# Attentions and mlps by 256 tokens, the first half beside the expert rows of the second

## What is computed

```python
def peer_ffn(u, w_q, sub_keys, expert_u, expert_v):
...
        ue = jnp.take(expert_u, expert, axis=0)
        ve = jnp.take(expert_v, expert, axis=0)
        h = jax.nn.gelu(jnp.einsum('thkd,td->thk', ue, xc).astype(F32), approximate=False)
        return jnp.einsum('thk,thkd->td', (gate * h).astype(xc.dtype), ve)
...
    for l in range(DEPTH_2):
...
            h = h + diff_attention(hn, w_qkv_a[l], w_o_a[l], lambda_q1[l], lambda_k1[l],
                                   lambda_q2[l], lambda_k2[l], subln_g[l], lambda_init,
                                   cos_a, sin_a)
...
            h = h + mla_attention(hn, w_dq[j], q_norm_g[j], w_uq[j], w_o_b[j],
                                  k_nope, k_rope, v, cos_b, sin_b)
        h = h + sq_relu_mlp(rms_norm(h, mlp_norm_g[l]), w_up[l], w_down[l])
    return rms_norm(h, final_norm_g)
```

## Time and profile before

| | us |
|---|---|
| median of 3 runs | 3588.33 |
| lowest, highest | 3582.31, 3590.96 |
| the profiled execution | 3589.93 |
| its span, first to last instruction | 3588.1 |
| TensorE busy | 2908.2 |
| DVE busy | 2067.9 |
| POOL busy | 1356.3 |
| ACT busy | 691.9 |
| mean granted TensorE clock | 0.921 |

### The profile page before, as it was taken

One profiled execution on the slowest core, in us unless ns is written; L12 is line 12 of the kernel. 1 busy time (PEld: TensorE's weight loads), 2 busy tenths in 40 slices (PEclk: granted clock), 3 DMA queues, 4 the chain that ended last, 5 costly groups with the idle time before them and its releaser, 6 DMA issues.

```text
span 3588.1 us, 31787 instructions
## 1 busy us (share of the span) xinstructions
PE 2908.2 (81%) x11588; PEld 1975.4 (55%) x11588; DVE 2067.9 (58%) x4063; ACT 691.9 (19%) x1259; POOL 1356.3 (38%) x764
## 2 busy tenths in 40 slices
PE   4954798695777777787777765999799997899998
PEld 3743788573332332333222222786688886677887
DVE  6798543446785777678665544336453444455334
ACT  2101222121000000000000002234232233343221
POOL 3833222245454444444444423320144442123442
PEclk9966999797999999999999987987799998899999
DMA  6210001125999999999999973210022213112221
GB/s 256 94 47 12 1 1 41 54 106 220 421 419 421 401 421 409 403 422 408 420 421 421 419 309 132 71 71 1 28 94 102 94 48 115 36 50 92 94 98 43
DMA packets 97691, 692.13 MB, mean 193 GB/s; under 512 B 10752, under 2 KB 10880, under 8 KB 14848
## 3 DMA queue, kind: packets, MB, share of 16 engines
q0 software_dynamic: 73728, 536.90, 36.3%
q1 hardware_dynamic: 23808, 153.20, 11.8%
HBM read 687.96 MB, written 2.10 MB: 192 GB/s over the span
## 4 chain that ended last, share of the span: by engine, by line
PE 53%; DMA 22%; DVE 16%; issue 5%; POOL 2%; ACT 2%; DVEq 0%; SPq 0%; ACTq 0%; POOLq 0%
PE ps L1775 10%; DMA w<-in_peer_uv,un 9%; PE ps L306 8%; PE ps L1623 8%; PE ps L1754 8%; DMA raw<-in_peer_uv,un 7%; PE ps L781 5%; DMA un<-in_peer_uv,un 5%; DVE scratch L559 4%; PE ps L2037 3%; PE ps L1967 2%; PE ps L2059 1%; DVE scratch L1678 1%; PE ps L1945 1%; PE ps L335 1%
## 5 line engine op out<-in xcount | busy, mean ns | idle before, releaser
L276 POOL TENSOR_TENSOR wl<-raw,wh 128x2048 fp32r<-128x2048 f32 (+2 forms) x118 | 530.9, 4507 | 1122.1 <-ACT wh L270 1121.9
L1623 PE MATMUL ps<-w,un 128*128 128x512 f32 x856 | 415.4, 632 | 159.3 <-DVE un L1686 159.3
L1623 PE MATMUL ps<-raw,un 128*128 128x512 f32 x768 | 376.6, 638 | 121.6 <-DVE un L1686 121.6
L1623 PEld LDWEIGHTS ps<-w,un 128*128 128x128 f32 x856 | 164.2, 200 | 405.3 <-DVE un L1686 228.9
L1678 DVE SCALAR_TENSOR_TENSOR scratch<-w,scratch 128x1024 f32<-128x1024 f32 x214 | 265.8, 1253 | 184.1 <-DMA w<-in_peer_uv,un 184.1
L1611 POOL DMA_INDIRECT w<-in_peer_uv,un x214 | 248.5, 1161 | 320.7 <-PE ps L1623 294.5
L1623 PEld LDWEIGHTS ps<-raw,un 128*128 128x128 f32 x768 | 147.9, 202 | 347.1 <-DVE un L1686 189.7
L1611 POOL DMA_INDIRECT raw<-in_peer_uv,un x192 | 235.8, 1228 | 263.9 <-PE ps L1623 251.3
L1678 DVE SCALAR_TENSOR_TENSOR scratch<-raw,scratch 128x1024 f32<-128x1024 f32 x192 | 232.8, 1223 | 137.8 <-DMA raw<-in_peer_uv,un 137.5
L1651 ACT ACTIVATE un<-un 128x2 f32<-128x2 f32 x256 | 52.1, 203 | 1224.5 <-DVE scratch L1678 1224.4
L270 ACT CAST wh<-raw 128x2048 fp32r<-128x2048 f32 (+2 forms) x118 | 216.9, 1851 | 317.4 <-PE ps L1775 194.7
(11 more groups left out here) (385 smaller groups left out, 5256.6 us busy)
## 6 DMA issues: line engine op xcount, KB each, us to landing
raw<-in_w_up SPq DMA_DIRECT2D x32, 1024.0 KB, 4.8
raw<-in_w_down SPq DMA_DIRECT2D x32, 1024.0 KB, 4.8
scratch<-in_ada_w SPq DMA_DIRECT2D x13, 1024.0 KB, 14.6
raw<-in_w_qkv_a SPq DMA_DIRECT2D x12, 1024.0 KB, 5.3
raw<-in_w_in SPq DMA_DIRECT2D x11, 1024.0 KB, 5.6
raw<-in_ada_w SPq DMA_DIRECT2D x11, 1024.0 KB, 4.8
raw<-in_peer_w_q SPq DMA_DIRECT2D x8, 1024.0 KB, 7.0
raw<-in_w_out SPq DMA_DIRECT2D x4, 1024.0 KB, 6.0
```

Of the source, the lines that this page charges most:

```text
L276: e.tensor_tensor(self.wl[h][:, 0:width], self.raw[slot][:, 0:width], self.wh[h][:, 0:width].bitcast(F32), ALU.subtract).then_inc(*self.ti ...
L1623: ins = e.matmul(self.ps[:, b + half, :], self.diag[n % 8], self.rows[self.row_of(n)][:, 1024 + 512 * half:1536 + 512 * half], start=k == ...
```

## The change

**Two halves.** The tail is written anew for 256 tokens (`Half`, `h` = 0 or 1) and runs twice, one half after the other (`pe_tail` and its siblings). Matmuls, activations and DVE instructions are 256 columns wide. The weight tiles are 128 x 1024 (in part 768), 184 per half, and every half loads, casts and splits all of them, through four `raw` buffers and four slots, in the mlps seven. The keys and values of half 0 go to HBM and come back for half 1. POOL's part in the double norm goes to DVE.

**Rows.** The first 256 rows run beside the three choices, 2.6 rows per step (`with_rows`, `beside`). The last 256 run beside the tail of half 0, 1.1 rows per unit of its weight (a unit is 24 matmuls of 256 columns; a step of attention counts 1.2; the whole is 242 units). From row 236 on there are six buffers. The rows' products change engine: the diagonal is made on ACT; of the last 256 rows three in four are multiplied and summed on DVE into SBUF (`acc`) and one in four on TensorE (`on_pe`), and DVE adds the two sums up (`dve_sums`). ACT makes Gelu and gate for one row at a time, in two instructions. POOL's splits stand between its row transfers, as soon as the slot is free by the order of turns (`spot`).

```diff
-LAST_RAW = 480
+FEW_ROWS = 236
+RATE = 1.1
...
+         "w_qk": (1024, 16, 8), "w_v": (1024, 8, 4), "w_o_a": (1024, 8, 8), "w_dkv": (1024, 3, 8), "ukv_k": (1024, 2, 2),
+         "ukv_v": (1024, 2, 2), "w_dq": (1024, 3, 8), "uq_n": (768, 4, 3), "uq_r": (768, 2, 3), "w_o_b": (1024, 8, 8),
+         "w_up_0": (1024, 32, 8), "w_up_1": (1024, 32, 8), "w_down_0": (1024, 32, 1), "w_down_1": (1024, 32, 1)}
...
+    for h in range(2):
+        for key in tail_keys(h):
+            plan[key] = (len(plan), 4 + len(plan) % 4, None)
...
+        slots = (4, 5, 6, 7, 8, 9, 10) if name[0:4] in ("w_up", "w_do") else (4, 5, 6, 7)
+        slot = min(slots, key=lambda s: -1 if last[s] is None else plan[last[s]][0])
+        before[key], last[slot] = last[slot], key
+        plan[key] = plan[key][0:2] + (slot,)
...
-        return n % 10 if n < LAST_RAW else (n - LAST_RAW) % 6
+        return n % 10 if n < FEW_ROWS else 4 + (n - FEW_ROWS) % 6
...
+    def on_pe(n):
+
+        return n < 256 or n % 4 == 3
...
-    def with_gather(self, choose, gather):
-
-        for tt in range(1, 4):
-            for n, _ in enumerate(choose(tt)):
-                for _ in range(2 if n % 2 else 1):
-                    next(gather)
-            for _ in range(64 - 46):
-                next(gather)
-        for _ in gather:
...
+    def beside(self, stage, rows, rate):
+
+        due = 0.0
+        for weight in stage:
+            self.turn += 1
+            due += rate * (weight or 1)
+            while due >= 1:
+                next(rows, None)
+                due -= 1
...
+    def with_rows(self, choose, rows, tail):
+
+
+        early = itertools.islice(rows, 257)
+        self.beside(itertools.chain(choose(1), choose(2), choose(3)), early, 2.6)
+        for _ in early:
             pass
+        self.banks, self.nbank = 6, 0
+        self.beside(tail(self.halves[0]), rows, RATE)
+        for _ in rows:
+            pass
+        self.banks, self.nbank = NBANK, 0
+        for _ in tail(self.halves[1]):
+            self.turn += 1
...
+            while n >= FEW_ROWS + 12 and at < len(lows) and self.spot_before(lows[at]) <= self.spot.get(("row", before), 0):
+                self.pool_lo(e, lows[at])
+                at += 1
...
+        e.activation(self.gelus[:, c], self.dots[:, c], ACT.Gelu, bias=0.0, scale=1.0).then_inc(*self.tick(S))
+        e.wait_ge(*self.last(S))
+        e.activation(self.weight[:, c], self.gelus[:, c], ACT.Identity, bias=0.0,
+                     scale=self.gate[n // 128][:, k:k + 1]).then_inc(*self.tick(S, ("weight", n)))
...
+            e.activation(self.diag[self.diag_of(n)], self.C("ident"), ACT.Identity, bias=0.0,
+                         scale=self.weight[:, c]).then_inc(*self.tick(S, ("diag", n)))
...
-                e.tensor_scalar(self.diag[n % 8], self.C("ident"), self.gelus[:, n % 256:n % 256 + 1],
-                                self.gate[tt][:, k:k + 1], ALU.mult, ALU.mult).then_inc(*self.tick(S, ("diag", n)))
...
+                    e.wait_ge(*self.at(S, ("acc", n - 1 if not self.on_pe(n - 1) else n - 2)))
+                    e.scalar_tensor_tensor(out=acc, in0=v, scalar=w, in1=acc, op0=ALU.mult,
+                                           op1=ALU.add).then_inc(*self.tick(S, ("acc", n)))
...
+            if n == 384:
+                self.dve_sums(e, 2)
...
+        blocks = [(hh, qb) for hh in range(8) for qb in (2 * H.h, 2 * H.h + 1)]
...
+                        for n, (l, r) in enumerate(self.terms(wh[:, k, :], wl[:, k, :], *H.B[k])):
+                            ins = e.matmul(self.ps[:, b, 0:256], l, r, start=k == 0 and n == 0, stop=k == 7 and n == 2)
...
+        yield from self.pe_joined(e, H)
+        yield from self.pe_diff(e, H)
+        yield from self.pe_mlp(e, H, 0)
+        yield from self.pe_mla(e, H)
+        yield from self.pe_mlp(e, H, 1)
+        yield from self.pe_final(e, H)
```

1591 lines of the change are left out of this document (865 added, 726 removed).

## The result

The changed kernel takes 3847.9 us (median; 3843.0 to 3850.4) against 3585.3 for the kernel before: 1.074 times as long, 95% interval 1.070 to 1.079. 3690 had been forecast, slower by 2.8%. The sign was right and the time lies in the range, but the loss was given as 105 us and is 263. The profiled execution took 3849.6 us, its span 3847.8.

The account below looks back on a forecast made before the run. DMA bound the rows and TensorE the tail, in series; side by side, the DVE/POOL port would bind. 1515 us to the 256th row + 1336 stage + 835 tail 1 = 3686, rounded 3690 with surroundings; range 3450 to 3870.

Parts of the forecast that it names:

- The bound before, and what both halves share: Rows bound by DMA, tail by TensorE, in series; side by side, DVE's two-SBUF-tensor instructions and POOL's splits exclude each other.
- The sum of 1135 us: Second rows beside tail 0: 542 us of dots and sums, 433 of splits, 160 of the half tail's DVE instructions, added.
- 256th row at 1515: First 256 rows run as before to 1510 us, plus 5 us for six buffers from row 236.
- Resources: Second rows beside tail 0, each resource's sum: DMA 871 us, TensorE 700, POOL 740, DVE 850.
- what doesn't pack: Second rows beside tail 0, added to the port's sum: attention 81 us, latencies 40, order 80.
- Order: POOL, ACT and TensorE wait for one another: 46 us per mlp group, 8% above the sum, 80 us in all.
- Tail 1 835: Last 256 tokens alone: 526 us matmuls, 154 attentions, 123 latencies, 32 splits; 835 us, between 800 and 880.
- split bursts: Tail 1's mlps: splits arrive in bursts of five, 13 us within 11.5, costing 2 us a group, 32 in all.
- the port doesn't add up: Rival: splits slip between dots or DVE's sums are free; stage some 1070 us, end 3425; chance 0.17.
- it packs well: Rival: port times add but order costs nothing; stage 1220 us, whole 3547, deciding at 1238 for the stage; chance 0.15.
- The third: Rival: TensorE's lower clock makes groups 56 us, whole 3850; or dots wait for POOL's row issues, 3930; chance 0.16.

Follow-up runs that it names:

- e1: Changed kernel with POOL splitting only 64 of 1024 columns for nearly every tail weight tile; 3512.1 us, 0.981 of the kernel before.
- e4: Changed kernel with all 368 splits of the tails' weights on DVE in place of POOL; 3813.0 us, 1.065 of the kernel before.
- e2: Changed kernel with RATE 0: the last 256 rows run behind the first half tail, not beside it; 3836.2 us, 1.072 of the kernel before.
- e12: Changed kernel with splits of 64 columns and dots and weights of rows 256 to 511 one row further ahead; 3413.5 us, 0.954 of the kernel before.
- e15: Changed kernel: first tail's and three of eight later splits on DVE, every second late row on TensorE, dots one row ahead, Gelu per two rows; 3567.3 us, 0.996.
- e5: Changed kernel with dots and weights of rows 256 to 511 two rows further ahead; 3837.8 us, 1.071 of the kernel before.
- e3: Changed kernel with all of rows 256 to 511 summed on TensorE, not one in four; 3825.0 us, 1.070 of the kernel before.

## Why the prediction was right or wrong

- **The bound before, and what both halves share.** Right. The step "DVE and POOL exclude each other, so their times add" is what e1 shows, 294 us of holding on DVE in the stage. The sum of 1135 us was 1082, so 5% too high. Of the signs named, mlp groups at 50.5 us for 46, DMA at 69% for 65 and 84 table loads for some 80 came near; dots and sums had means of 1.48 and 1.90 us and a longest of 4.1, for 2 and over 5.
- **256th row at 1515.** 1520. The splits of the tail's first four tiles were not in the step. POOL ran them in one go ahead of a row's issue, and a dot was held until they were over (in e4, where DVE splits them later, the dot of row 256 starts at 1512.5 us, here at 1520.3). DVE's work up to there was 474 us for 480, though no row shows the 110 us in its working, where its own subtraction gives 73:

```profile
1479.47 10.91 DVE L1748 SCALAR_TENSOR_TENSOR scratch<-un,scratch 128x1024 f32<-128x1024 f32 x1 [1.25 <-DMA un<-in_peer_uv,un]
...
1480.07 9.23 POOL L297 TENSOR_TENSOR wls<-raws,whs 128x1024 fp32r<-128x1024 f32 x4
```

- **Resources.** DVE 850: 827 in e1. POOL 740: 786 as it ran, its own waiting included. TensorE 700: 891; e2 has 670 of it for the tail alone and 240 for the 64 rows, which is 3.75 us a row at a granted clock of 0.59, in place of the 2.0 of before. DMA: 369 MB for 362. None of these sums is as long as the stage.
- **The step that failed: what doesn't pack.** The terms of 81 + 40 + 80 = 201 us measured 401. "Order", 8% on the bound resource, was the worst. The 16 groups of the mlps were to take 736 us, 678 of port and 58 beside it (46 a group, 3.6 of it beside the port); they took 809, 630 of port and 179 beside it (11.2 a group). The attentions, 213 us with 81 beside the port, took 242 with 125 beside it. The rest, with 62 beside the port, had 97. The port's term was 53 us too high and hid part of this; 200 less 53 is the 147 us by which the stage was missed. What stands in place of a percentage is a ring of waits of its own: TensorE waits for a row's diagonal, ACT for its dot, DVE behind a split or an activation. TensorE stands in it for 20 us of each group. e12 measures a part of it with the port nearly out of the way: one row of lead, 99 us.
- **Tail 1 835.** 845. Its groups took 27.2 us for 25; 97 us of it hang on the splits (e1), not 32 as "split bursts" had it. Other terms were too high by some 55 us, the attentions among them (135 for 154). So 835 was near by two errors that offset each other.
- **What should have been asked, and wasn't.** The forecast set the stage against its resources, and never against its two parts run one behind the other. By its own terms these are 645 us for the transfers and 526 + 71 + 123 + 32 = 752 for the half tail (71 being 225 less 154 of attention), 1397 together. So even the forecast's 1336 left an overlap of only 61 us, against the 190 that halving costs by the same terms (752 + 835 less 1397.5). Measured, the parts are 652 + 815 = 1467 and halving costs 263.
- **The rivals.** The first (the port doesn't add up, 3425) falls by e1. The second (it packs well, 3547) did not come: 1483 us for 1220. Its point of decision, 1238 us of stage, went with 835 us behind it; e15 is ahead of before with 1242 because 808 stand behind it. The third had the right number, 3850, by another cause. A group's matmuls were to take 46 us by themselves at the lower level of the clock; TensorE was busy for 31 us of a group at a granted 0.79, and for 29 in e12 at 0.90, while its waits went from 20 us to 7. Its other half, row issues that hold DVE, falls too: in e4, with 251 issues beside them, no dot took over 1.28 us.
- **Who blocks whom.** The Trainium skill (page "SBUF — State Buffer", section "Who interferes with whom") says that the shared ports are an exclusive lock and that the order of issue decides who blocks. The trace agrees in the main: of 76 dots and sums that started inside a split 75 were held, and 80 splits that started inside a dot or a sum took 2.77 us in the median (up to 3.35) for some 2.4. But ten dots that by the trace started 0.2 to 0.6 us ahead of a split were held by it all the same, the one of 10.91 us among them. All ten began during the row issue that stands before the split on POOL, as here; no run shows why, since a row issue with no split behind it holds no dot (e4):

```profile
1662.23 1.77 POOL L1639 DMA_INDIRECT raw<-in_peer_uv,un  x1
...
1663.49 3.97 DVE L1748 SCALAR_TENSOR_TENSOR scratch<-un,scratch 128x1024 f32<-128x1024 f32 x1
1664.03 2.35 POOL L297 TENSOR_TENSOR wls<-raws,whs 128x1024 fp32r<-128x1024 f32 x1
```

- **Interleaving.** The Trainium skill (page "Perfetto Trace Analysis", section "Optimization Strategy") says that a kernel whose busiest engine changes from stage to stage may be improved by interleaving the stages. By that rule the stage may have come out shorter than its parts; here it was 16 us longer. It took 1242 us only once splits, order and the rows' products had been changed, and the parts of that kernel were not run one behind the other.

Open: e1 and e12 leave most of the low parts out of what they compute; they price the splits and are no kernels to use. What a group in e15 (41.6 us) has above e12's 37.4 is DVE's splits or its order, and no run tells which. One row of lead beside POOL's splits was not run; two rows were (e5). What the granted clock costs was not isolated by any run.

## What to carry to other kernels

Before two stages are laid side by side, price them one behind the other, in the form in which they will run; here having the tail in two halves cost 263 us before anything overlapped. Then look for what they share that no busy share shows, such as the port between POOL and DVE, and for which engine's program order ties them together. Two such causes can cover each other: the lead that alone moved the whole by 10 us brought 75 us of stage beside e4's edit and, as one row in place of two, 99 us beside e1's, so try them together before dropping one.

## What the hardware showed

- The same subtraction of 1024 columns takes POOL 2.35 to 2.50 us and DVE 1.21. With all splits of a tail on DVE nothing was held (e4: no dot over 1.28). Beside rows that was the better place (46.5 us a group for 50.5); for the last 256 tokens, where POOL has nothing else to do, it was the worse one (30.4 for 27.2).
- An instruction of two SBUF tensors that is held gets next to nothing done until the split, and the splits that follow at once, are over: one dot took 10.9 us across four splits and ended 1.1 us behind the last.
- The granted clock was 0.59 in e2's rows alone (TensorE busy for 240 of 652 us), 0.77 in the stage with rows (891 of 1483) and 0.90 in e3's (1177 of 1461). In the six groups above it rose from 0.79 to 0.90 when TensorE's waits were taken away, and TensorE's busy time went from 31 to 29 us a group: here the low clock went with waiting, and explains at most some 2 us of the 14 between the two.
